# The end of a top-16 search on VectorE: comparison, product and sum, or exclusive or and minimum

## The reference, cut to what matters

```python
q = (xb @ w_query).reshape(t, PEER_HEADS, 2, HALF_KEY)
s = jnp.einsum('thik,hink->thin', q, sub_keys)
v_half, i_half = lax.top_k(s, TOPK)                       # 16 of 128 keys, in each half
cand = (v_half[:, :, 0, :, None] + v_half[:, :, 1, None, :]).reshape(t, PEER_HEADS, TOPK * TOPK)
cand_idx = (i_half[:, :, 0, :, None] * N_KEYS + i_half[:, :, 1, None, :]).reshape(...)
top_v, top_pos = lax.top_k(cand, TOPK)                    # 16 of 256 sums
idx = jnp.take_along_axis(cand_idx, top_pos, axis=-1)
g = jax.nn.softmax(top_v, axis=-1)
act = jax.nn.gelu(jnp.einsum('thkd,td->thk', expert_u[idx], xb))
return jnp.einsum('thk,thkd->td', (g * act), expert_v[idx])
```

## Time and profile before

| | us |
|---|---|
| median of 3 runs | 2580.18 (2577.29 to 2587.11) |
| the profiled execution | 2583.05 |
| its span | 2581.2 |
| busy PE | 2300.2 (89%) |
| busy DVE | 1797.7 (70%) |
| busy POOL | 1179.9 (46%) |
| busy ACT | 635.8 (25%) |

### The profile page before, as it was taken

How to read it: one execution, slowest core, us unless ns; L and a number is a source line. 1 busy time by engine, 2 the same in 40 slices (tenths; PEclk the granted TensorE clock), 3 DMA queues, 4 the chain that set the end, 5 groups by cost and what they waited for, 6 DMA issues and landing times.

```text
span 2581.2 us, 26507 instructions
## 1 busy us (share of the span) xinstructions
PE 2300.2 (89%) x8779; PEld 1451.1 (56%) x8779; DVE 1797.7 (70%) x3184; ACT 635.8 (25%) x1564; POOL 1179.9 (46%) x979
## 2 busy tenths in 40 slices
PE   6988888898899997999989999978799999999960
PEld 1545454454566443487668887856566666644420
DVE  2657676645600789778778898899676767657678
ACT  2325435231211113411322112199111111110010
POOL 0022231221000346667542235477557786876865
PEclk8999999999999998999999999999899999999985
DMA  8211101107585678999874578999999999999997
GB/s 308 74 33 58 41 24 41 49 33 296 164 284 178 213 298 324 370 369 413 320 268 160 223 280 322 351 365 412 417 379 419 378 411 409 383 400 372 414 389 288
DMA packets 235577, 705.28 MB, mean 273 GB/s; under 512 B 22910, under 2 KB 47614, under 8 KB 234052
## 3 DMA queue, kind: packets, MB, share of 16 engines
q0 software_dynamic: 117936, 429.44, 43.1%
q1 hardware_dynamic: 116948, 272.27, 28.4%
q10 hardware_dynamic: 576, 2.10, 0.2%
HBM read 690.23 MB, written 13.50 MB: 273 GB/s over the span
## 4 chain that ended last, share of the span: by engine, by line
PE 31%; DVE 22%; POOL 17%; DMA 15%; issue 11%; ACT 3%; SPq 1%; DVEq 0%; ACTq 0%; POOLq 0%
PE bank L960 13%; POOL arena L1785 7%; POOL arena L1777 7%; DMA arena<-in_peer_v,arena 6%; DMA arena<-in_peer_u,arena 6%; PE bank L809 4%; PE bank L854 2%; DVE arena L2205 2%; DVE arena L2183 2%; DVE arena L1966 2%; PE bank L1112 2%; POOL arena L1834 2%; DVE arena L2129 2%; DVE arena L2126 2%; DVE arena L2128 1%
## 5 line engine op out<-in xcount | busy, mean ns | idle before, releaser
L1777 POOL DMA_INDIRECT arena<-in_peer_u,arena x384 | 489.1, 1274 | 577.7 <-DVE arena L2183 326.5
L2205 DVE SCALAR_TENSOR_TENSOR arena<-arena 128x1024 f32<-128x1024 f32 x381 | 495.3, 1300 | 139.0 <-DMA arena<-in_peer_v,arena 134.3
L2183 DVE CUSTOM_DVE_ANT_0 arena<-arena 128x1024 f32<-128x1024 f32 x384 | 476.4, 1247 | 150.2 <-DMA arena<-in_peer_u,arena 149.6
L1785 POOL DMA_INDIRECT arena<-in_peer_v,arena x384 | 463.9, 1208 | 244.0 <-DVE arena L2205 136.8
L960 PE MATMUL bank<-arena 128*128 128x512 f32 (+1 forms) x1472 | 507.2, 507 | 15.3 <-DMA arena<-in_w_in 5.2
L1220 PE MATMUL bank<-arena 128*128 128x512 f32 x1024 | 452.3, 594 | 13.4 <-DVE arena L2381 9.3
L1182 PE MATMUL bank<-arena 128*128 128x256 f32 x2048 | 455.3, 380 | 7.1 <-ACT arena L1634 6.4
L1182 PEld LDWEIGHTS bank<-arena 128*128 128x128 f32 x2048 | 390.6, 191 | 88.4 <-issue 37.4
L960 PEld LDWEIGHTS bank<-arena 128*128 128x128 f32 x1472 | 282.4, 193 | 236.0 <-issue 201.1
L1220 PEld LDWEIGHTS bank<-arena 128*128 128x128 f32 x1024 | 195.0, 191 | 232.7 <-issue 214.4
L1634 ACT ACTIVATE arena<-bank 128x256 f32<-128x256 f32 x128 | 49.0, 383 | 589.4 <-PE bank L1182 589.4
(11 more groups left out here) (260 smaller groups left out, 2476.6 us busy)
## 6 DMA issues: line engine op xcount, KB each, us to landing
arena<-in_peer_ut SPq DMA_DIRECT2D x128, 512.0 KB, 6.5
arena<-in_peer_v SPq DMA_DIRECT2D x128, 512.0 KB, 6.6
arena<-in_w_in SPq DMA_DIRECT2D x22, 2048.0 KB, 8.1
arena<-in_w_ada_t POOLq DMA_DIRECT2D x32, 512.0 KB, 4.0
arena<-in_w_ssd_out SPq DMA_DIRECT2D x8, 2048.0 KB, 13.2
arena<-in_w_query SPq DMA_DIRECT2D x8, 2048.0 KB, 7.9
arena<-in_w_ada SPq DMA_DIRECT2D x4, 2048.0 KB, 16.3
arena<-in_w_fourier SPq DMA_DIRECT2D x4, 2048.0 KB, 7.7
```

Source lines behind the costliest of these rows:

```text
L1777: nc.gpsimd.indirect_dma_start(rowbuf[slot], None, a["peer_u"], bass.IndirectOffsetOnAxis(ap=entries(IDX, k), axis=0)).then_inc(row_in[slo ...
L1785: nc.gpsimd.indirect_dma_start(rowbuf[slot], None, a["peer_v"], bass.IndirectOffsetOnAxis(ap=entries(IDX, k), axis=0)).then_inc(row_in[slo ...
L2183: V.tensor_tensor_reduce(out=rowbuf[slot], in0=rowbuf[slot], in1=h2c if item < PH else h2a[:, item // PH - 1, :], scale=1.0, scalar=0.0, o ...
L2205: STT(pv, rowbuf[slot], w, pv, ALU.mult, ALU.add).then_inc(s("vc_used"), 1)
```

## The change

The numbers of the 16 best keys are stored as 16-bit integers that hold key + 128 m, m being the place from 0 to 15 (in place of a cast to bfloat16). The place found is scaled to 128 a and 128 b and stored twice, side by side. One exclusive or of the two gives the key number alone where the places are equal, and at least 128 elsewhere; a minimum over 16 then gives the key number. The result goes out as bfloat16 (whole numbers up to 127). Two small constants take the place of the table of places.

```diff
--- before.py
+++ after.py
@@ -13,6 +13,7 @@
 F32 = mybir.dt.float32
 BF16 = mybir.dt.bfloat16
 U32 = mybir.dt.uint32
+U16 = mybir.dt.uint16
 I32 = mybir.dt.int32
 ACT = mybir.ActivationFunctionType
 ALU = mybir.AluOpType
@@ -354,7 +355,8 @@
         selb = sb("selb", [P, HEADS], BF16)
         selg = sb("selg", [P, HG], BF16)
         stat = sb("stat", [P, 64])
-        places = sb("places", [P, 4, TOPK], U32)
+        places = sb("places", [P, 2, TOPK], U32)
+        key_place, shifts = places[:, 0, :], places[:, 1, 0:2].bitcast(F32)
         masks = sb("masks", [P, 2, TOPK], U32)
 
 
@@ -470,7 +472,7 @@
         tables_c = [at(125.75 + 0.5 * i, PICKS) for i in range(3)]
         tables_a = [at(kb, 2 * PICKS) for kb in (198, 199, 108)]
         ij_w = [at(kb, 2 * PICKS).rearrange("p (t n) -> p t n", t=2) for kb in (139.25, 140.25)]
-        ij_all = at(139.25, 4 * PICKS).rearrange("p (g n) -> p g n", g=4)
+        ij_all = at(139.25, 2 * PICKS).bitcast(BF16).rearrange("p (g n) -> p g n", g=4)
         d_w = at(109, 2 * PICKS).rearrange("p (t n) -> p t n", t=2)
         turned_w = at(131.25, 2 * P)
         features = at(132.25, FEATURES * P).bitcast(BF16).rearrange("p (t f k) -> p t f k", t=2, f=FEATURES)
@@ -497,10 +499,11 @@
         cands, cand2 = at(119, 512), at(121, 256)
         small = at(124, 12 * 32).rearrange("p (i n) -> p i n", i=12)
         four = at(122, 4 * 64).rearrange("p (i n) -> p i n", i=4)
-        v16s, i16s, tijs, picks = four[:, 0], four[:, 1].bitcast(U32), four[:, 2].bitcast(U32), four[:, 3]
+        v16s, i16s, tijs, picks = four[:, 0], four[:, 1].bitcast(U32), four[:, 2].bitcast(U32), four[:, 3].bitcast(BF16)
         small64 = at(124, 64)
         tvs, tps = small64[:, 0:32], small64[:, 32:64].bitcast(U32)
-        i16fs = small[:, 2].bitcast(BF16)
+        i16fs = small[:, 2].bitcast(U16)
+        tij16s = small[:, 3:5].rearrange("p a b -> p (a b)").bitcast(U16)
         dots = [small[:, 7, 0:TOPK], small[:, 11, 0:TOPK]]
         ge, ex = small[:, 7, TOPK:], small[:, 8, 0:TOPK]
         esum, erec = small[:, 9, 0:1], small[:, 9, 1:2]
@@ -1863,9 +1866,9 @@
             dve.wait_ge(s("consts_in"), 16 * len(CONSTS))
             CP(identb[:], ident)
             CP(selb[:], sel[:])
-            row16 = shp[:, 6, 0:TOPK].unsqueeze(1).broadcast_to([P, 2, TOPK])
-            CP(places[:, 2:4, :], row16)
-            TS(places[:, 0:2, :], row16, float(TOPK), None, ALU.mult)
+            TS(key_place, shp[:, 6, 0:TOPK], float(NKEY), None, ALU.mult)
+            V.memset(shifts[:, 0:1], float(NKEY // TOPK))
+            V.memset(shifts[:, 1:2], float(NKEY))
             V.memset(masks[:, 0, :], TOPK * (TOPK - 1))
             V.memset(masks[:, 1, :], TOPK - 1)
             V.memset(eps[:], EPS)
@@ -2151,7 +2154,7 @@
                     src = scores_of(item)
                     for half in range(2):
                         best16(v16[:, half, q, :], i16[:, half, q, :], src[:, half, :], sw2[:, half, :])
-                CP(i16fs[:, 0:2 * n * TOPK], i16s[:, 0:2 * n * TOPK])
+                TT(flat(i16fs), flat(i16s), key_place.unsqueeze(1).broadcast_to([P, 2 * n, TOPK]), ALU.add)
                 ch(TT(cand, v16[:, 0].unsqueeze(3).broadcast_to([P, n, TOPK, TOPK]),
                       v16[:, 1].unsqueeze(2).broadcast_to([P, n, TOPK, TOPK]), ALU.add))
                 for q in range(n):
@@ -2162,15 +2165,19 @@
                 TT(over, tv, tv[:, :, 0:1].broadcast_to([P, n, TOPK]), ALU.subtract)
                 ch(TT(tij, tp.unsqueeze(1).broadcast_to([P, 2, n, TOPK]), masks[:].unsqueeze(2).broadcast_to([P, 2, n, TOPK]),
                       ALU.bitwise_and))
-                e4 = cands[:, 0:256 * n].bitcast(BF16).rearrange("p (g k m) -> p g k m", g=2 * n, m=TOPK)
-                place = places[:, 0:4:3 - n, :]
-                ch(TT(e4, place.unsqueeze(2).broadcast_to([P, 2 * n, TOPK, TOPK]),
-                      flat(tijs).unsqueeze(3).broadcast_to([P, 2 * n, TOPK, TOPK]), ALU.is_equal))
-                ch(TT(e4, e4, flat(i16fs).unsqueeze(2).broadcast_to([P, 2 * n, TOPK, TOPK]), ALU.mult))
+                twice = tij16s[:, 0:4 * n * TOPK].rearrange("p (h q c) -> p h q c", h=2, c=2)
+                ch(TT(twice, tijs[:, 0:2 * n * TOPK].rearrange("p (h q) -> p h q", h=2).unsqueeze(3).broadcast_to([P, 2, n * TOPK, 2]),
+                      shifts.unsqueeze(2).unsqueeze(3).broadcast_to([P, 2, n * TOPK, 2]), ALU.mult))
+                e4 = cands[:, 0:256 * n].bitcast(U16).rearrange("p (g k m) -> p g k m", g=2 * n, m=TOPK)
+                by_two = [P, 2 * n, TOPK, TOPK // 2, 2]
+                ch(TT(e4.rearrange("p g k (m c) -> p g k m c", c=2),
+                      flat(i16fs).rearrange("p g (m c) -> p g m c", c=2).unsqueeze(2).broadcast_to(by_two),
+                      tij16s[:, 0:4 * n * TOPK].rearrange("p (g k c) -> p g k c", g=2 * n, c=2).unsqueeze(3).broadcast_to(by_two),
+                      ALU.bitwise_xor))
                 if t in WHOLE:
-                    V.tensor_reduce(ij_all[:, :, TOPK * h:TOPK * h + TOPK], e4, AX.X, ALU.add).then_inc(s("topw_done"), n)
+                    V.tensor_reduce(ij_all[:, :, TOPK * h:TOPK * h + TOPK], e4, AX.X, ALU.min).then_inc(s("topw_done"), n)
                 else:
-                    ch(V.tensor_reduce(flat(picks), e4, AX.X, ALU.add))
+                    ch(V.tensor_reduce(flat(picks), e4, AX.X, ALU.min))
                     half = picks[:, 0:n * TOPK], picks[:, n * TOPK:2 * n * TOPK]
                     STT(entries(IDX, items[0] * TOPK, n * TOPK), half[0], float(NKEY), half[1],
                         ALU.mult, ALU.add).then_inc(s("topk_done"), n)
```

## The result

The changed kernel takes 2596.33 us (median of 14 runs, 2582.70 to 2603.74), beside 2583.98 us for the kernel before on the same chips (14 runs, 2576.99 to 2591.19). The ratio is 1.0045, with a 95% interval of 1.0028 to 1.0062: about 0.5% slower, where 13 us faster was forecast. The profiled execution took 2603.74 us, the highest of its runs (span 2601.9).

What follows compares the result with a forecast made beforehand. PE's multiplications pace 1824 to 2490 us, with transfers full; earlier, PE stands twice because DVE is late. Gains 3.7 + 6.4 + 1.0 + 1.9 = 13.0 us take the median 2580.18 to 2567.2 us; 8 in 10: 2560 to 2579.

Steps and rivals of the forecast that it cites:

- the 0.05 for slower: Whole kernel: chance 0.05 of over 0.5% slower, above 2593 us, from late weights or a cost that no row shows.
- the tail of rows: After 2490 us only gathered rows are left; these 91 us were costed as unchanged.
- The exclusive or at 692 ns: In each pair search: the 16-bit exclusive or takes 692 ns, as the product it replaces; upper end 1225 ns.
- Rival 1: In the searches: the exclusive or does one result at a time, so 6.3 us gained, 2573.9 us; chance 0.12.
- A pair: One search of two together on VectorE: the new form saves 0.92 us, or 0.39 with a slow exclusive or.
- Before 985 us, 3.7 us: Five searches ahead of the 32nd dot product: PE, ACT and DVE enter the whole searches 3.7 us early.
- rival 2: Rows, not DVE's own work, set its pace: only 6.4 us of the gain stay, 2573.8 us; chance 0.22.
- PE's first gap: PE's wait for ACT at 984.6 us: it shrinks from 10.03 us by 3.7 to 6.3.
- From 1350 to 1824 us, 6.4 and 1.0: Ten pair searches remove PE's whole 6.38 us gap at 1581.2 us; DVE's further lead up to 1824 gains 1.0.
- VectorE's further lead at the gates: From 1680 to 1824 us: of DVE's 4.6 us lead, 1 us counts as gained, bounds 0 and 4.6.
- From 1824 us on, 1.9: Four searches in the last stage: row work gains 1.9 us, half of 3.7, bounds 0 and 3.7.
- Rival 3: From 1100 to 1240 us: rows run ahead delay weight loads and PE waits; slower, 2587 us; chance 0.06.

Runs made afterwards that it cites:

- the kernel with the filler: New search with the arena at 24064, plus additions that nothing needs, two in each pair search; 2586.09 us, ratio 1.0006 of the kernel before.

## Why the prediction was wrong, step by step

**The step that failed: what the change moves.** The sum counted VectorE's instructions only. The smaller `places` had no term in it, neither a cost nor a bound, though the earlier trace rows name the resource that it touches: transfers at a share of 1.00 for 810 us. The list of terms was incomplete; no term was mis-sized by this. The only room left for it was the 0.05 for slower, "a cost that no row shows". The price is 20 to 26 us (23.4 and 25.7 with the old search, 20 to 26 with the new), most of it in the last stage: there the four aligned profiles with the new search have a mean of 753.3 us, the changed kernel 774.3 and 769.0 (mean 771.6). That is 2.4% of the stage, near the 2.8% of the transfers alone. It comes out in the tail of rows, which the prediction costed as unchanged. The forecast of 2567.2 us is, within 4 us, the time of the change with the arena aligned (2569.24, 2569.97, 2570.79).

The Trainium skill has the rule that I didn't look at from this side: DMA: Bandwidth & Descriptors, "How a descriptor splits into AXI transactions", says by the vendor's account that a descriptor is cut into transactions of 256 bytes which must start on a multiple of 256, and that one which starts off it also fetches the bytes before its start, at a cost in beats of 32 bytes. It speaks of reading, and gives no times. That being off by 32, 64 or 128 bytes costs time and 256 bytes nothing agrees. For 4 KB pieces the rule gives 17 transactions in place of 16, an estimated 6.25%. By its beats it gives 132 in place of 128 for 128 bytes off, an estimated 3.1%, but only 129, or 0.8%, for 32 bytes off. Measured are 2.8% for landings, with 44.18 and 43.98 us at 32 bytes off hardly less than the 44.12 to 44.26 at 128, then 3.0% for stores 128 bytes off and about 2.4% in the last stage, and the measurement decides. Neither count fits all of it, and what sets the size stays open.

**The exclusive or at 692 ns: right.** Rival 1 is out. A pair takes 0.93 us less (3.49 to 2.55), where 0.92 was forecast. The Trainium skill's Vector Engine (DVE) Microarchitecture Reference, section 5.2, that spoke against it with 1.4 us or more, isn't borne out by this row.

**Before 985 us, 3.7 us: too large.** Summed over the rows of VectorE's timeline from the first search to ACT's turn, its busy time did fall, from 130.4 to 130.7 us (three profiles with the old search) to 127.0 to 127.3 (four with the new one), by 3.4. The stage shrank by 0.8 us only (means 138.8 and 138.1), which the spread hardly lets one tell from nothing (138.08 to 139.72, and 137.73 to 138.51). Most of the rest came back as waits, which grew from a mean of 14.8 us to 17.1. VectorE in order of time, new search, arena where it was:

```profile
902.83 0.69 DVE L2080 TENSOR_TENSOR arena<-arena 128x512 f32<-128x512 f32 x1 [1.73 <-ACT arena L1324]
```

This wait for ACT is in three of the four profiles (1.45 to 1.73 us) and in none of the three with the old search: VectorE comes to that product before ACT has copied its operand out of PE's bank. In the fourth the rows take it (13.65 us of waits for DMA in the stretch, in place of 10.3 to 12.0). So the chain was held by ACT's copy or by rows, and only the second is rival 2. PE's first gap is 8.04 to 8.83 us in the four and 8.40 to 10.03 in the three, where 6.3 was forecast. This rests on the profiles; the time of the kernel with the new search in the context tile only, 0.3 to 8.5 us below before, doesn't decide between 0.8 and 3.7.

**From 1350 to 1824 us, 6.4 and 1.0: the mechanism right, the sizes not.** The scores' stage is shorter by 9.0 us in every profile, to the hundredth of a microsecond the same without the gap. The gap is 6.38 of them; the other 2.6 are the clock. The kernel before in stretches of 2 us behind the gap (columns as in the earlier trace rows):

```profile
1586.00:1588.00 2.00, 0.42 (x1) 0.46 (x2) 1.23 (x3) 1.97 (x3) 1.70 (x2) 0.50 0.86 246
1588.00:1590.00 2.00, 2.00 (x6) 1.56 (x6) 0.84 (x3) 1.98 (x4) 1.70 (x2) 0.50 0.79 238
1590.00:1592.00 2.00, 2.00 (x7) 1.56 (x6) 1.31 (x3) 0.82 (x3) 1.19 (x2) 0.50 0.90 287
1592.00:1594.00 2.00, 2.00 (x10) 1.79 (x9) 0.90 (x3) 0.38 (x1) 0.94 (x1) 0.93 0.96 330
1594.00:1600.00 6.00, 6.00 (x30) 5.28 (x29) 3.34 (x6) 0.38 (x1) 3.94 (x4) 1.00 0.79 289
```

and the new search with the arena at 24064, at the same time:

```profile
1590.00:1600.00 10.00, 10.00 (x48) 8.82 (x47) 5.45 (x10) 1.15 (x3) 7.87 (x8) 1.00 1.01 407
```

When PE took up its work at 1587.58 the granted clock was 0.50, its lower level of 1.2 GHz, and stayed there to some 1592: 6 or 7 products in 2 us in place of 10. Nearly 5 us of work at half the rate lose about 2.5. I priced the gap and not what it does to the clock behind it, though the 0.97 of that stage stands in the earlier trace rows. VectorE's further lead at the gates, taken as 1.0, gave 0.4 (means 141.7 and 141.3), less than the 1.4 by which the three profiles with the old search differ.

**From 1824 us on, 1.9: inside its bounds, but not shown.** The means differ by 2.5 us (755.8 and 753.3), between the bounds of 0 and 3.7. But the two profiles of the kernel before differ by 3.0, and the kernel with the filler, which gives the saving back, took 754.7.

So the aligned change gains 0.8 + 9.0 + 0.4 + 2.5 - 0.2 (the second stage of the table) = 12.5 us by the stages, and 11.4 to 12.7 by the ratios of the three kernels that hold it (0.9951 to 0.9956), against the forecast of 13.0. That the sum agrees is partly luck: one term too large by 2.9, one too small by 2.6. Only the 9.0 us stand clear of the spread between profiles.

**Rival 3, slower by late weights.** A wait of 0.76 us for in_w_ssd_out at 1189.34 us does appear in the changed kernel, the sign that I had named for it. It isn't its proof: the old search with the arena moved has one too (0.88 at 1215.39), and so have the other two profiles off a multiple of 256, so it needs no lead of VectorE. Of the four aligned profiles with the new search ahead of it one also has such a wait, 1.07 us at 1213.88, and of the three with the old search there one, 0.57 us at 1207.03; whether a lead adds to it can't be told from that.

## What to carry to other kernels

Read a diff for what it does to addresses, not to instructions alone: a table that gets smaller moves all that is allocated behind it, and where transfers are the bound, an address off a multiple of 256 bytes cost 2 to 3% of that time here. The firm sign in the trace was the same bytes at fewer GB/s where the transfers are full (390 to 392 in the four profiles off it, 399 to 402 in the eight on it); slower work ahead of the first changed instruction was a hint that needed more than one profile. The cheap test is to pad the allocation back. And a gap on PE is worth more than its length when the granted clock drops behind it, while a shorter chain on VectorE is worth less than its busy time when the next thing that it needs comes at its own pace.

## What the runs showed of the hardware

- Destinations in SBUF off a multiple of 256 bytes by 32, 64 or 128 bytes: 44.18 us for 16 MB in pieces of 4 KB, against 42.96 us on it (380 against 390 GB/s). Multiples of 512 were not measurably better than those of 256.
- Sources in SBUF 128 bytes off: five stores of 512 KB to HBM in 7.81 us, against 7.58 on the multiple.
- Behind a gap of 6.38 us PE ran at a granted clock of 0.50 for nearly 5 us; without the gap the stage was 9.0 us shorter.
- An exclusive or of 16-bit integers in adjacent pairs, one operand returning eight times to the same pair, runs as fast as a bf16 product: 692 ns for 1024 results.
- A minimum over 1024 numbers of 16 bits takes what a sum over bf16 does, 1220 ns.
- The scaling from 32-bit to twin 16-bit numbers: 291 ns for 128 results.
